# ScalarE takes the ranking's key copies, the index tiles' copies out of PSUM and the statistics of the last LayerNorm

## The chip, the cores and the metric

The kernel runs on one core of one Trainium2 chip, as one launch. The metric is the device time of that launch in microseconds, median of several runs. TensorE (PE) multiplies, VectorE (DVE) and ScalarE (ACT) work on tiles in SBUF and PSUM, GpSimd (POOL) issues the gathers of expert rows, SyncE (SP) issues the large loads and stores.

## What is computed

One layer of a streaming encoder for 1024 tokens of width 1024: an input projection with two mixers, a residual LayerNorm, and then a product-key expert layer (PEER) with another residual LayerNorm. The change touches only the expert layer and the last LayerNorm:

```python
def block(xb):                       # PEER
    q = (xb @ w_q).reshape(t, PEER_HEADS, 2, PEER_HALF)
    s = jnp.einsum('thpd,hpkd->thpk', q, sub_keys)
    s1, i1 = lax.top_k(s[:, :, 0], PEER_TOPK)
    s2, i2 = lax.top_k(s[:, :, 1], PEER_TOPK)
    cand_s = (s1[..., :, None] + s2[..., None, :]).reshape(t, PEER_HEADS, 256)
    cand_i = (i1[..., :, None] * PEER_N_KEYS + i2[..., None, :]).reshape(t, PEER_HEADS, 256)
    top_s, sel = lax.top_k(cand_s, PEER_TOPK)
    idx = jnp.take_along_axis(cand_i, sel, axis=-1)
    gate = jax.nn.softmax(top_s, axis=-1)
    act = jax.nn.gelu(jnp.einsum('thkd,td->thk', expert_u[idx], xb))
    return jnp.einsum('thk,thkd->td', gate * act, expert_v[idx])
...
x = LN(alpha * x + gate2(c) * PEER(h2)) * ln2_g + ln2_b
```

There are 8 heads, 128 keys a half, 16 chosen of each, and 16384 experts.

## The kernel before

**Two token sets.** The 1024 tokens are worked as set A (3 blocks of 128) and set B (5 blocks, 640 tokens). A's expert rows are gathered one by one from memory (GpSimd, `row_at` buffers) and multiplied in by VectorE (`u_row`, L1067, and `v_row`, L1076). B's experts are computed densely: TensorE multiplies B's tokens with all of `expert_u` (64 units "E") and, after a one-hot spread of the gates, with all of `expert_v` (64 units "W").

**Units.** All weights pass as units of 1 MB, in the order of the list UNITS: A's front (V, C, U, M, O), then B's with A's query units between (`B V`, `B C 0`, `A Q 0`, `B C 1`, ...), then `B U`, `B M`, `B O`, `B Q 0`, `B Q 1`, then five E units and one Q unit in turns up to `B Q 7`, then E 30 to E 63, then W. Every matrix product is three fp16 products (high by high, high by low, low by high). A unit is loaded into `stage` by SP, ScalarE writes its high part (`make_hi`, L726 to `w`), VectorE the low part (`make_lo`, L971), four units ahead of TensorE. For B a feature unit has 96 matmuls in 4 tiles of 24, 320 columns each; the tiles go round four PSUM banks, `psU`, so that TensorE may start a tile once ScalarE has copied out the tile four before it (`evacuate`, semaphore `tile_free`). The transposes, scores and spreads use four other banks, `psX`, released by `x_free`.

**Order.** There is no scheduler: each engine's program is written out in the loop over UNITS, and runs in that order. In each unit ScalarE copies the unit's tiles out, then the scores of the head before, then does `make_hi(n + 4)`, then the store of an E unit and the gelu of the row dots (`section_gelu`, which waits for VectorE's rows of two sections earlier). VectorE does `make_lo(n + 4)`, then some pieces of the ranking, then the rows of the unit (`rows_of`).

**Ranking.** `rank(x, h)` is a generator of six pieces for one head: piece 1 the first eight of 16 best scores, piece 2 the second eight and the indices as fp16 (`idx16`, L1318, which raises `sc_used`), piece 3 the first half of the best sums, piece 4 the second half and the places, and pieces 5 and 6 the lookup of the two indices: an `is_equal` of places with a counter (L1359), a multiplication with the indices (L1362), four additions. L1362 reads `idx16` with a broadcast last axis. In the E units head `1 + (u - 1) // 5` has pieces 1 and 2 at u % 5 == 1 and one piece in each unit after it; from u = 33 two. Head 0 of B has its first three pieces at `B Q 1` and the others at E 0.

**The way to the spread.** E_SPREAD is 40. After E 38 TensorE transposes six tiles (two index arrays and the gates, each in two parts) into `psX`, and VectorE copies them out (`idx_t`, L1413 and L1415) into `keys_t16` and `g_t`. From E 40 on VectorE makes one-hot tiles (`onehot_keys`, L1430, and `onehot_gate`, L1437; eight pairs a unit, q counts them), and TensorE multiplies them after the 9th and the 21st matmul of each tile (L1831). Gathers of the phase "spread" (from E 40) wait until the first L1430 is done.

**The end.** In `close(i, b)` VectorE finishes one block after the other, in the order 0, 1, 3, 4, 2, 5, 6, 7: it scales the sum (L1607 from SBUF for A's blocks, L1620 twice from PSUM for B's), adds the residual (L1622), takes the statistics (L1625, L996, L999), waits for ScalarE's square root (L756), and normalises (L1004, L1629, L1631). Three of B's ten output tiles share one PSUM bank and are copied out by `shared_out` (L1574), which releases the bank to TensorE.

## Time and profile before

| | us |
|---|---|
| median of three timed runs | 3033.12 (3030.32 to 3034.49) |
| the profiled execution | 3017.38 |
| its span, first to last instruction | 3015.6 |
| TensorE busy | 2903.5 |
| VectorE busy | 2554.3 |
| ScalarE busy | 836.3 |

The mean granted TensorE clock is 0.990 of full speed. A busy TensorE means here that matmuls follow one another; its idle stretches are few, and each has a row of its own in the timeline with the idle time and what ended it.

### The profile page before, as it was taken

The page shows a single profiled execution, that of the slowest core. Times are in us where ns is not written, and L with a number is a line of the kernel's source. Part 1 is how long each engine was busy: PE and PEld are TensorE (multiplying, and loading weights), DVE is VectorE, ACT ScalarE, POOL GpSimd, SP SyncE. Part 2 cuts the span into 40 slices and gives each one's busy share as a digit, 9 for nine tenths or more (in the row PEclk, how much of TensorE's full clock was granted, in tenths as well). Part 3 has the DMA queues.
Part 4 walks back from the last instruction along what each step waited for, and adds up shares of the span by engine and source line. Part 5 has one row for each costly group of instructions (what it writes and reads, how often), then busy time and mean ns, then how long its engine had stood idle before and what let it go on. Part 6 is the DMA issues. An engine that isn't in the chain of part 4 may idle for free.

```text
span 3015.6 us, 47305 instructions
## 1 busy us (share of the span) xinstructions
PE 2903.5 (96%) x19184; PEld 1916.8 (64%) x19184; DVE 2554.3 (85%) x4745; ACT 836.3 (28%) x1245; POOL 1007.8 (33%) x778
## 2 busy tenths in 40 slices
PE   4999999998999899999999899999999999999997
PEld 3666686676677776777777688888644444444443
DVE  5886557997887689999999888887699999999878
ACT  3333431211111422222223233333322222222220
POOL 0000000003775025555444422222366556555410
PEclk9999999999999999999999999999999999999999
DMA  8899644334999269888898888889899999999972
GB/s 329 336 350 369 213 171 164 128 105 182 393 393 358 91 238 340 315 329 333 316 351 305 299 287 294 285 285 294 334 415 415 410 399 406 398 409 401 348 276 104
DMA packets 266234, 917.53 MB, mean 304 GB/s; under 512 B 20464, under 2 KB 102432, under 8 KB 222752
## 3 DMA queue, kind: packets, MB, share of 16 engines
q1 hardware_dynamic: 63968, 427.91, 36.7%
q0 software_dynamic: 110592, 402.70, 35.5%
q10 hardware_dynamic: 91456, 83.89, 8.5%
q8 instruction: 152, 2.49, 0.3%
q14 instruction: 66, 0.54, 0.0%
HBM read 771.79 MB, written 142.63 MB: 303 GB/s over the span
## 4 chain that ended last, share of the span: by engine, by line
PE 54%; DVE 20%; issue 13%; DMA 10%; POOL 2%; ACT 1%; SPq 0%; DVEq 0%; ACTq 0%; POOLq 0%
PE psU L1651 11%; PE psU L1652 11%; PE psU L1653 11%; PE psX L1831 5%; PE psX L1651 5%; PE psX L1653 5%; PE psX L1652 5%; DVE acc_sp L1076 3%; DVE w L971 3%; DMA stage<-in_w_front 3%; DMA Z<-in_v_rows,idx_sp 2%; DMA rows<-in_v_rows,idx_sp 2%; DVE rows L1067 1%; POOL rows L719 1%; DMA rows<-in_u_rows,idx_sp 1%
## 5 line engine op out<-in xcount | busy, mean ns | idle before, releaser
L1651 PE MATMUL psU<-hB,w 128*128 128x320 f16 (+2 forms) x3104 | 931.7, 301 | 27.6 <-ACT Z L726 14.6
L1652 PE MATMUL psU<-hB,w 128*128 128x320 f16 (+2 forms) x3104 | 928.5, 300 | 0.0
L1653 PE MATMUL psU<-hB,w 128*128 128x320 f16 (+2 forms) x3104 | 928.2, 300 | 0.0
L971 DVE SCALAR_TENSOR_TENSOR w<-stage,w 128x2048 f16<-128x2048 f32 x176 | 402.8, 2289 | 115.6 <-ACT w L726 115.6
L726 ACT ACTIVATE w<-stage 128x2048 f16<-128x2048 f32 x176 | 335.9, 1909 | 544.1 <-PE psX L1653 349.5
L719 POOL DMA_INDIRECT rows<-in_u_rows,idx_sp x200 | 269.9, 1350 | 398.2 <-DVE rows L1067 253.1
L1651 PEld LDWEIGHTS psU<-hB,w 128*128 128x128 f16 x3104 | 308.5, 99 | 140.6 <-issue 20.6
L1653 PEld LDWEIGHTS psU<-hB,w 128*128 128x128 f16 x3104 | 305.4, 98 | 118.2
L1652 PEld LDWEIGHTS psU<-hB,w 128*128 128x128 f16 x3104 | 308.6, 99 | 111.2
L719 POOL DMA_INDIRECT rows<-in_v_rows,idx_sp x205 | 256.4, 1251 | 306.8 <-DVE rows L1067 209.3
L1651 PE MATMUL psX<-w,Z 128*128 128x512 f16 x768 | 291.1, 379 | 5.9 <-DVE Z L1574 4.3
L1652 PE MATMUL psX<-w,Z 128*128 128x512 f16 x768 | 291.1, 379 | 0.0
L1653 PE MATMUL psX<-w,Z 128*128 128x512 f16 x768 | 291.1, 379 | 0.0
L1651 PE MATMUL psU<-w,Z 128*128 128x512 f16 (+1 forms) x768 | 265.9, 346 | 9.6 <-DVE Z L1042 4.3
L1076 DVE SCALAR_TENSOR_TENSOR acc_sp<-rows,weight_sp,acc_sp 128x1024 f32<-128x1024 f32 x205 | 258.2, 1291 | 13.3 <-DMA rows<-in_v_rows,idx_sp 10.7
L1653 PE MATMUL psU<-w,Z 128*128 128x512 f16 (+1 forms) x768 | 265.8, 346 | 0.0
L1652 PE MATMUL psU<-w,Z 128*128 128x512 f16 (+1 forms) x768 | 265.7, 346 | 0.0
L1067 DVE SCALAR_TENSOR_TENSOR rows<-rows,h_sp 128x1024 f32<-128x1024 f32 x200 | 239.7, 1220 | 18.4 <-DMA rows<-in_u_rows,idx_sp 17.1
L726 ACT ACTIVATE R<-psU 128x320 f32<-128x320 f32 (+1 forms) x296 | 125.8, 429 | 424.7 <-PE psU L1653 424.4
L726 ACT ACTIVATE Z<-psU 128x320 f32<-128x320 f32 (+3 forms) x228 | 98.9, 447 | 471.7 <-PE psU L1653 423.8
L1651 PE MATMUL psU<-Z,w 128*128 128x384 f16 (+1 forms) x640 | 205.8, 322 | 0.0
L1652 PE MATMUL psU<-Z,w 128*128 128x384 f16 (+1 forms) x640 | 205.7, 321 | 0.0
(252 smaller groups left out, 4543.5 us busy)
## 6 DMA issues: line engine op xcount, KB each, us to landing
stage<-in_u_units SPq DMA_DIRECT2D x64, 1024.0 KB, 9.0
stage<-in_v_units SPq DMA_DIRECT2D x64, 1024.0 KB, 7.8
stage<-in_w_front SPq DMA_DIRECT2D x48, 1024.0 KB, 8.2
hl_dram<-w SPq DMA_DIRECT2D x48, 1024.0 KB, 6.3
w<-hl_dram SPq DMA_DIRECT2D x48, 1024.0 KB, 7.2
a_dram<-R ACTq DMA_DIRECT2D x64, 640.0 KB, 9.4
g_dram<-Z ACTq DMA_DIRECT2D x20, 2048.0 KB, 15.3
Z<-a_dram SPq DMA_DIRECT2D x32, 1280.0 KB, 11.6
```

What stands on the lines that cost most here:

```text
L719: pool.indirect_dma_start(row_at[r], None, u_rows if table == "u" else v_rows, bass.IndirectOffsetOnAxis(ap=idx_sp[:, slot:slot + 1], axis ...
L726: return nc.scalar.activation(dst, src, func, scale=scale)
L971: V.scalar_tensor_tensor(w[:, n % NW, 1, :], stage[:, v % 2, :], WS, w[:, n % NW, 0, :], ALU.mult, ALU.subtract).then_inc(lo_done, 1)
L1067: V.scalar_tensor_tensor(row_at[r], row_at[r], 1.0, h2_sp[:, slot % SB, :], ALU.mult, ALU.mult, accum_out=dots[:, c % 8, j:j + 1]).then_in ...
L1076: V.scalar_tensor_tensor(dst, row_at[r], weight_sp[:, slot:slot + 1], dst, ALU.mult, ALU.add).then_inc(row_used, 1)
L1651: mm(ps, lhs[0](k), rhs[0](k), start=start and s == 0, stop=False)
L1652: mm(ps, lhs[0](k), rhs[1](k), start=False, stop=False)
L1653: last = mm(ps, lhs[1](k), rhs[0](k), start=False, stop=stop and s == n - 1)
L1831: ins = mm(ps[:, t * P:(t + 1) * P], oh_keys[:, q % 4, 0, :, t], oh_gate[:, q % 4, c, :, t], start=(c == 0), stop=(c == 1))
```

## The change

Four edits, all in the programs of the engines:

1. **Keys.** A new `spread_keys` on ScalarE copies the 16 indices of each half into a full array `keys16` (16 by 16 a block), two ACTIVATEs a head: for A's heads 0 to 6 at the units of the table SPREAD_A, for B's head 0 at E 0, for B's head 1 + u // 5 at the E units with u % 5 == 2. It waits for `sc_used`, that is for the head's piece 2. VectorE multiplies with `keys16` instead of the broadcast `idx16`, after a wait on `keys_spread`; A's head 7 stays as it was.
2. **Index tiles.** ScalarE copies the six tiles out (`indices_out`): four after its `make_hi` at E 38, two in the middle of E 39. TensorE transposes four after E 38 and the two gate tiles inside E 39. VectorE's `idx_t` now stands after its rows of E 39 instead of before its rows of E 38.
3. **Rows.** In E 40 the first four pairs of one-hot tiles have no row between them; what is left of the rows follows at the unit's end.
4. **End.** `close` is cut in two: `close_sum` up to the residual, and `close` from the reciprocal on, done one block later. In between ScalarE makes the statistics: a Copy with its sum, the negative mean, a Square with its sum, and the square root.

```diff
+SPREAD_A = {("A", "Q", 1): 0, ("B", "C", 3): 1, ("A", "Q", 3): 2, ("B", "C", 6): 3, ("A", "Q", 5): 4,
+            ("B", "C", 9): 5, ("A", "Q", 7): 6}
...
+            def spread_keys(x, h):
+                k = rk[x]
+                act.wait_ge(sc_used, (HEADS if x == "B" else 0) + h + 1)
+                for half in range(2):
+                    dst = k["keys16"][:, half, :].rearrange("p (b j k) -> p b j k", b=NBLK[x], j=TOPK)
+                    activation(dst, k["idx16"][:, :, half, :].unsqueeze(3).to_broadcast([P, NBLK[x], TOPK, TOPK])
+                               ).then_inc(keys_spread, 1)
...
                 make_hi(n + NW)
+                if (x, kind, u) == ("B", "E", 0):
+                    spread_keys("B", 0)
+                if (x, kind, u) in SPREAD_A:
+                    spread_keys("A", SPREAD_A[x, kind, u])
+                if kind == "E" and u % 5 == 2 and u < E_SPREAD - 4:
+                    spread_keys("B", 1 + u // 5)
...
+                if (x, kind, u) == ("B", "E", E_SPREAD - 2):
+                    act.wait_ge(row_used, RANK_ROWS)
+                    indices_out(0, 4)
...
             for i, b in enumerate(CLOSE_ORDER):
-                root(R_END + i, slice(b, b + 1))
+                at, y = slice(b, b + 1), y_end[i % 2]
+                act.wait_ge(sum_ready, i + 1)
+                nc.scalar.activation(y, x_end[b], ACT.Copy, accum_out=total[:, at]).then_inc(act_step, 1)
+                act.wait_ge(act_step, 3 * i + 1)
+                activation(neg_mean[:, at], total[:, at], ACT.Copy, -1.0 / D).then_inc(act_step, 1)
+                act.wait_ge(act_step, 3 * i + 2)
+                nc.scalar.activation(y, x_end[b], ACT.Square, bias=neg_mean[:, at], accum_out=squares[:, at]
+                                     ).then_inc(act_step, 1)
+                act.wait_ge(act_step, 3 * i + 3)
+                nc.scalar.activation(std[:, at], squares[:, at], ACT.Sqrt, bias=end_eps[:, :], scale=1.0 / D
+                                     ).then_inc(std_ready, 1)
...
-                    step(V.tensor_tensor(cmp_t, cmp_t, k["idx16"][:, :, half, :].unsqueeze(3).to_broadcast([P, nb, TOPK, TOPK]),
-                                         ALU.mult))
+                    if (x, h) == ("A", HEADS - 1):
+                        keys = k["idx16"][:, :, half, :].unsqueeze(3).to_broadcast([P, nb, TOPK, TOPK])
+                    else:
+                        dve.wait_ge(keys_spread, 2 * (done - (x == "B")) - 1 + half)
+                        keys = k["keys16"][:, half, :].rearrange("p (b j k) -> p b j k", b=nb, j=TOPK)
+                    step(V.tensor_tensor(cmp_t, cmp_t, keys, ALU.mult))
...
-                        if q % 2:
+                        if q % 2 and q > 4:
                             next(rest, None)
...
-                if kind == "E" and u == E_SPREAD - 2:
-                    idx_t()
...
                     rows_of(unit)
+                    if kind == "E" and u == E_SPREAD - 1:
+                        idx_t()
...
-                step(V.scalar_tensor_tensor(x_end[b], x_end[b], ALPHA, y, ALU.mult, ALU.add))
-                settle()
-                for half in range(2):
-                    step(V.bn_stats(stats[:, b, half, :], x_end[b][:, half * HT:(half + 1) * HT]))
-                settle()
-                aggregate(range(b, b + 1), 2)
+                V.scalar_tensor_tensor(x_end[b], x_end[b], ALPHA, y, ALU.mult, ALU.add).then_inc(sum_ready, 1)
+
+            def close(i, b):
                 inverse(R_END + i, range(b, b + 1))
...
-                close(i, b)
+                close_sum(i, b)
+                if i:
+                    close(i - 1, CLOSE_ORDER[i - 1])
+            close(NB - 1, CLOSE_ORDER[-1])
```

ScalarE's program in E 1, E 2 and E 3, before (`R<-psU` are a unit's four tiles, `w<-stage` is `make_hi`, `dots` the gelu, the DMA the unit's store):

```order
L726 ACTIVATE R<-psU 128x320 x4
L929 DMA a_dram<-R 128x1280
L726 ACTIVATE dots<-dots 128x2
L726 ACTIVATE R<-psU 128x320 x4
L726 ACTIVATE w<-stage 128x2048
L929 DMA a_dram<-R 128x1280
L726 ACTIVATE dots<-dots 128x2
L726 ACTIVATE R<-psU 128x320 x4
```

and now:

```order
L974 DMA a_dram<-R 128x1280
L739 ACTIVATE dots<-dots 128x2
L739 ACTIVATE R<-psU 128x320 x4
L739 ACTIVATE w<-stage 128x2048
L739 ACTIVATE Z<-Z 128x1280 x2
L974 DMA a_dram<-R 128x1280
L739 ACTIVATE dots<-dots 128x2
L739 ACTIVATE R<-psU 128x320 x4
```

The two key copies of B's head 1 (`Z<-Z`) stand between `make_hi` of E 2 and the four tiles of E 3.

VectorE's program from its last rows of E 38 to the first one-hot tiles of E 40, before (L1067 and L1076 are rows, L1430 and L1437 the one-hot pair; the copies L1413 and L1415 and the casts L1419 to L1422 stand a few instructions further up, between `make_lo` and the rows of E 38):

```order
L1076 SCALAR_TENSOR_TENSOR acc_sp<-rows,weight_sp,acc_sp 128x1024 x2
L1089 SCALAR_TENSOR_TENSOR weight_sp<-dots,gate_sp 128x3
L1067 SCALAR_TENSOR_TENSOR rows,dots<-rows,h_sp 128x1024
L1067 SCALAR_TENSOR_TENSOR Z,dots<-Z,h_sp 128x1024
L1076 SCALAR_TENSOR_TENSOR acc_sp<-rows,weight_sp,acc_sp 128x1024 x2
L1089 SCALAR_TENSOR_TENSOR weight_sp<-dots,gate_sp 128x2
L1430 TENSOR_TENSOR Z<-Z 128x1024
L1437 TENSOR_TENSOR Z<-Z 128x1024
L1430 TENSOR_TENSOR Z<-Z 128x1024
L1067 SCALAR_TENSOR_TENSOR Z,dots<-Z,h_sp 128x1024
L1437 TENSOR_TENSOR Z<-Z 128x1024
```

and now:

```order
L1132 SCALAR_TENSOR_TENSOR acc_sp<-rows,weight_sp,acc_sp 128x1024 x2
L1145 SCALAR_TENSOR_TENSOR weight_sp<-dots,gate_sp 128x2
L1469 CAST Z<-Z 128x640
L1471 TENSOR_TENSOR Z<-Z 128x640
L1472 CAST Z<-iota_i 128x512
L1480 TENSOR_TENSOR Z<-Z 128x1024
L1487 TENSOR_TENSOR Z<-Z 128x1024
L1480 TENSOR_TENSOR Z<-Z 128x1024
L1487 TENSOR_TENSOR Z<-Z 128x1024
L1480 TENSOR_TENSOR Z<-Z 128x1024
```

The copies out of PSUM are gone from it, the rows come ahead of the casts, and no row stands between the first one-hot pairs.

ScalarE's last instructions are now, for the first and the second block:

```order
L1000 ACTIVATE Z,total<-Z 128x1024
L739 ACTIVATE neg_mean<-total 128x1
L1004 ACTIVATE Z,squares<-Z,neg_mean 128x1024
L1007 ACT_TABLE_LOAD
L1007 ACTIVATE std<-squares,end_eps 128x1
L1000 ACTIVATE Z,total<-Z 128x1024
L739 ACTIVATE neg_mean<-total 128x1
L1004 ACTIVATE Z,squares<-Z,neg_mean 128x1024
L1007 ACTIVATE std<-squares,end_eps 128x1
```

One table is loaded for all eight blocks.

## Rows read from the trace of the kernel before

**Rows 1.** The page's busy times: us, share of the span, instructions.

```profile
PE 2903.5 (96%) x19184; PEld 1916.8 (64%) x19184; DVE 2554.3 (85%) x4745; ACT 836.3 (28%) x1245; POOL 1007.8 (33%) x778
```

**Rows 2.** Timeline, TensorE: start, duration (us), instruction, idle time before it, releaser.

```profile
681.83 0.58 PE L1706 MATMUL psX<-Z,R 128*128 128x128 f32 x1 [4.05 <-DVE Z L1197]
...
1149.91 0.30 PE L1651 MATMUL psU<-hB,w 128*128 128x320 f16 x1 [2.91 <-ACT Z L726]
...
1679.42 0.77 PE L1847 MATMUL psX<-ident,Z 128*128 128x128 f32 x5 [4.64 <-DVE Z L1413]
...
1703.93 0.52 PE L1831 MATMUL psX<-Z 128*128 128x128 f16 x3 [4.34 <-DVE Z L1437]
...
2975.31 0.39 PE L1651 MATMUL psX<-w,Z 128*128 128x512 f16 x1 [3.10 <-DVE Z L1574]
...
3001.00 0.38 PE L1653 MATMUL psX<-w,Z 128*128 128x512 f16 x1
```

**Rows 3.** Busy time by stretches: length, PE, PEld, DVE, ACT, POOL, PEclk, DMA share, GB/s.

```profile
680.10:686.80 6.70, 4.97 (x20) 3.63 (x21) 4.09 (x9) 0.00 (x0) 0.00 (x0) 0.50 0.00 1
1151.20:1154.50 3.30, 3.30 (x14) 1.86 (x13) 3.06 (x18) 0.00 (x0) 0.53 (x1) 0.50 0.99 387
```

**Rows 4.** Groups by line and shape, VectorE: count, busy us, mean ns, idle before.

```profile
L1362 DVE TENSOR_TENSOR Z<-Z 128x1280 f16<-128x1280 f16 x16 | 23.9, 1492 | 0.6
L1362 DVE TENSOR_TENSOR acc_sp<-acc_sp 128x768 f16<-128x768 f16 x16 | 15.3, 958 | 0.6
L1359 DVE TENSOR_TENSOR Z<-Z,iota_jk 128x1280 f16<-128x1280 f16 x16 | 13.0, 814 | 0.1
L1359 DVE TENSOR_TENSOR acc_sp<-acc_sp,iota_jk 128x768 f16<-128x768 f16 x16 | 8.9, 558 | 0.6
```

**Rows 5.** The same of ScalarE.

```profile
L726 ACT ACTIVATE w<-stage 128x2048 f16<-128x2048 f32 x176 | 335.9, 1909 | 544.1 <-PE psX L1653 349.5 <-DMA stage<-in_w_front 121.0 <-DMA stage<-in_u_units 73.6
L798 ACT ACTIVATE hB<-Z 128x1024 f32<-128x1024 f32 x1 | 1.1, 1057 | 3.5 <-DMA Z<-in_c_row 3.5
```

**Rows 6.** Timeline, VectorE, in the rankings (columns as in rows 2).

```profile
643.53 0.17 DVE L1166 COPY Z<-carry 128x4 f32<-128x4 f32 x1 [2.63 <-ACT Z L726]
...
1128.57 0.24 DVE L1318 CAST Z<-Z 128x160 f16<-128x160 uint32 x1
...
1210.43 0.24 DVE L1318 CAST Z<-Z 128x160 f16<-128x160 uint32 x1
```

**Rows 7.** Timeline, ScalarE, in E 2, E 3 and at E 7.

```profile
1107.32 0.44 ACT L726 ACTIVATE R<-psU 128x320 f32<-128x320 f32 x1 [2.82 <-PE psU L1653]
1107.65 1.90 ACT L726 ACTIVATE w<-stage 128x2048 f16<-128x2048 f32 x1
...
1120.36 0.44 ACT L726 ACTIVATE R<-psU 128x320 f32<-128x320 f32 x1 [2.82 <-PE psU L1653]
...
1194.11 1.91 ACT L726 ACTIVATE w<-stage 128x2048 f16<-128x2048 f32 x1 [0.54 <-DMA stage<-in_u_units]
```

**Rows 8.** Timeline, VectorE, from `make_lo` at E 38 to the first one-hot tile.

```profile
1676.61 2.29 DVE L971 SCALAR_TENSOR_TENSOR w<-stage,w 128x2048 f16<-128x2048 f32 x1
...
1695.37 0.68 DVE L1430 TENSOR_TENSOR Z<-Z 128x1024 f16<-128x1024 f16 x1
```

**Rows 9.** The chain that ended last, two gathers: issued, us until landed.

```profile
1661.44 13.87 DMA rows<-in_v_rows,idx_sp
...
1687.78 6.30 DMA rows<-in_v_rows,idx_sp
```

**Rows 10.** Timeline, VectorE, the first block's end and the last instruction.

```profile
2954.50 1.23 DVE L1622 SCALAR_TENSOR_TENSOR Z<-Z 128x1024 f32<-128x1024 f32 x1
2955.76 1.29 DVE L1625 BATCH_NORM_STATS2 stats<-Z 128x6 f32<-128x512 f32 x2
...
2957.83 1.27 DVE L1629 SCALAR_TENSOR_TENSOR Z<-Z,mv,h_sp 128x1024 f32<-128x1024 f32 x1
...
3011.24 1.28 DVE L1631 SCALAR_TENSOR_TENSOR hB<-hB,rstd,h_sp 128x1024 f32<-128x1024 f32 x1
```

More of the change, by code:

```diff
@@ L320, in trunk_layer @@
         unread = sb("unread", [P, 1])
+        end_eps = sb("end_eps", [P, 1])
+        total = sb("total", [P, NB])
+        neg_mean = sb("neg_mean", [P, NB])
+        squares = sb("squares", [P, NB])
         dots = sb("dots", [P, 8, 12])
@@ L497, in trunk_layer @@
         sc_used = sem("sc_used")
+        keys_spread = sem("keys_spread")
         s_shift = sem("s_shift")
@@ L513, in trunk_layer @@
         v_free = sem("v_free")
+        sum_ready = sem("sum_ready")
+        act_step = sem("act_step")
         y_ready = sem("y_ready")
@@ L790, in scores, with indices_out @@
                     activation(flat[:, HT * i:HT * i + n], psX[a % 4][:, 0:n]).then_inc(x_free[a % 4], 1)
+            def spread_keys(x, h):
[5 more added lines that the diff above has]
+                               ).then_inc(keys_spread, 1)
+            def indices_out(lo, hi):
+                for i in range(lo, hi):
+                    kind, (first, last) = i // 2, SPLIT["B"][i % 2]
+                    a = X_IDX + i
+                    n, at = (last - first) * P, slice(first * P, last * P)
+                    wait_x(act, a)
+                    if kind < 2:
+                        activation(keys_t16[:, kind, at], psX[a % 4][:, 0:n]).then_inc(x_free[a % 4], 1)
+                    else:
+                        activation(g_t[:, at], psX[a % 4][:, 0:n], ACT.Copy, GS).then_inc(x_free[a % 4], 1)
             def section_gelu(n):
@@ L908, in _ @@
                             evacuate(t + 2 * j + half, slot[:, j, half * HB:(half + 1) * HB], ACT.Gelu_apprx_tanh)
+                            if u == E_SPREAD - 1 and 2 * j + half == 1:
+                                indices_out(4, 6)
                 if (x, kind, u) == ("A", "C", 5):
@@ L1118, in _ @@
             step(V.memset(modc[:, :], 0.0))
+            step(V.memset(end_eps[:, :], EPS))
             dve.wait_ge(tanh_c, 1)
@@ L1404, in idx_t @@
             def idx_t():
-                dve.wait_ge(row_used, RANK_ROWS)
-                for i in range(6):
-                    kind, (lo, hi) = i // 2, SPLIT["B"][i % 2]
-                    a = X_IDX + i
-                    n = (hi - lo) * P
-                    at = slice(lo * P, hi * P)
-                    wait_x(dve, a)
-                    if kind < 2:
-                        V.tensor_copy(keys_t16[:, kind, at], psX[a % 4][:, 0:n]).then_inc(x_free[a % 4], 1)
-                    else:
-                        V.tensor_scalar(g_t[:, at], psX[a % 4][:, 0:n], GS, None, ALU.mult).then_inc(x_free[a % 4], 1)
                 for i in range(4):
@@ L1764, in q_scores, with index_tiles @@
                     ins.then_inc(x_ready, 1)
+            def index_tiles(lo, hi):
+                for i in range(lo, hi):
+                    flat = (i1_all, i2_all, s_all)[i // 2]["B"].rearrange("p b h k -> p b (h k)")
+                    first, last = SPLIT["B"][i % 2]
+                    ps = x_tile(X_IDX + i)
+                    for b in range(first, last):
+                        ins = nc.tensor.transpose(ps[:, (b - first) * P:(b - first + 1) * P], flat[:, b, :], ident[:, :])
+                    ins.then_inc(x_ready, 1)
             pe.wait_ge(ident_ready, 2)
@@ L1834, in _, with gates_between @@
                     feature_unit(n, hl, spread)
+                elif (x, kind, u) == ("B", "E", E_SPREAD - 1):
+                    def gates_between(r, s):
+                        if (r, s) == (1, 2):
+                            pe.wait_ge(gate_ready, 2)
+                            index_tiles(4, 6)
+                    feature_unit(n, hl, gates_between)
                 else:
@@ L1839, in _ @@
                 if (x, kind, u) == ("B", "E", E_SPREAD - 2):
[L1840 to L1849 removed]
+                    pe.wait_ge(s_shift, 2)
+                    index_tiles(0, 4)
             first_w = N_OF["B", "W", 0]
```

16 lines of the change are left out of this document (4 added, 12 removed).

## The prediction

> **What bounds the kernel now.** I read the page's busy times first: TensorE is at 96% of the span, VectorE at 85%, ScalarE at 28% [rows 1]. So work that leaves VectorE shortens the kernel only where TensorE stands waiting for it, and work put on ScalarE costs only where TensorE comes to wait for ScalarE. The next view is TensorE's timeline with the idle time in front of each instruction. The waits that the edits can reach are few [rows 2]: 4.05 us at 681.83 (VectorE, the mixer's tiles), 2.91 at 1149.91 (ScalarE, which had not copied out a tile), 4.64 at 1679.42 (the index tiles in PSUM), 4.34 at 1703.93 (the second one-hot pair), 3.10 at 2975.31 (the shared PSUM bank). Behind such waits the granted clock is 0.50 for a while, 1.2 instead of 2.4 GHz [rows 3]: 3.3 us behind the wait that ends at 1149.91, which costs half of that, 1.65; behind the one that ends at 681.83 until 686.8, 5.0 us, which costs 2.5. Last, the end: TensorE's last matmul starts at 3001.00 [rows 2], VectorE's last instruction ends at 3012.52 [rows 10]. There VectorE sets the end.
>
> **Own time and median.** The sum is made on the profiled execution: span 3015.6, its time 3017.38. The median of the timed runs is 15.7 us higher, with no part of it in this view; I carry the difference over unchanged.
>
> **1. Keys on ScalarE, set A.** The multiplication with a broadcast operand takes 0.958 us at 768 columns and 1.492 at 1280; the comparison of the same size, with whole rows in its last axis, 0.558 and 0.814 [rows 4]. I take these for the new multiplication: 0.40 and 0.68 saved a half, 0.8 and 1.36 a head. Of A's seven heads nearly all of it is lost: at 643.53 VectorE has caught up and waits 2.63 us for tiles of TensorE's pace [rows 6]. Only head 6 comes after it, so VectorE comes 0.8 us earlier to the wait that ends at 681.83, and TensorE's next wait behind it is one for VectorE's chain as well. Term: **-0.8** (0 to -2, the latter if the slow clock gets shorter too).
>
> **2. Keys on ScalarE, set B.** ScalarE's 1024 columns take 1.057 us, its 2048 columns 1.909 [rows 5], so 0.832 ns a column; 1280 columns are 1.27, two copies about 2.5 us. In idle time they are free. But they stand behind a wait. At E 2 ScalarE is through with `make_hi` at 1107.65 + 1.90 = 1109.55 [rows 7] and now waits for `sc_used` of head 1. VectorE is two units behind here: that cast ends at 1128.57 + 0.24 = 1128.8 [rows 6], less 1.36 for head 0 is 1127.45. With the copies ScalarE is back at 1130.0. Queued behind it are the four tiles of E 3. TensorE finishes the fourth at 1120.2 (ScalarE's copy of it starts at 1120.36 [rows 7]) and can't start E 4 before the first is copied out, at 1130.5. **TensorE stands still for about 10.3 us**, and a slow clock of 1.65 to 2.5 follows; I take 2.1. What goes in return: VectorE catches up during the standstill, so the 2.91 us at 1149.91 and its 1.65 of clock are gone. Counted through: a unit of 96 matmuls takes 13.04 us (from the last tile's copy at 1107.32 to that at 1120.36 [rows 7]). E 4 and the query unit behind it take two times that, so E 5 starts at 1130.5 + 26.1 + 2.1 = 1158.7 instead of 1149.91 + 1.65 = 1151.55. Term: **+7.1** (+5.5 to +9). Head 0 at E 0 does not do this: ScalarE waits there about 5 us, with 3 us left before TensorE needs a bank. From E 5 to E 38 TensorE has no wait before and I expect none.
>
> **3. Index tiles and first one-hot pairs.** Before: 4.64 us of wait, 4.34 at the second pair [rows 2], and behind each the same 3.3 us of slow clock as behind the one at 1149.91, 1.65 of cost each: 12.3 in all with nothing between but E 39. Now TensorE passes E 38 without a stop: ScalarE frees the banks, and E 39 starts at 1674.7 and ends, with five transposes in it, at 1688.2, in the frame of the old trace. It wants the first pair at 1689.4. VectorE's `make_lo` of E 38 started at 1676.61 [rows 8] and can't be over 0.6 earlier, since ScalarE's half ends at 1676.0. Then come 2.2 us, the four rows of E 38, four rows of E 39, and the casts, 1.75. The rows of E 39 hang on gathers: the two of the nearest kind took 6.3 us in a quiet stretch and 13.9 under a 1 MB load [rows 9], and the gathers of E 39 are now issued while the load of that unit runs (1678 to 1687). I take 9 us for the first of the last three, issued at 1679.8, and 1.3 more for each next: rows done at 1692.2, casts at 1694.0, first pair at 1695.4 instead of 1696.8 (1695.37 and two instructions [rows 8]). So TensorE waits here again, some 6 us, with 2.2 of clock. The gain is the second pair: no row, which had waited for its gather, stands in front of it. It starts 2.6 us behind the first, and the point of full speed comes at 1695.5 + 2.6 + 2.2 = 1700.3 instead of 1703.93 + 1.65 = 1705.6. Term: **-5.3** (-2.5 with gathers of 13 us, -9 with gathers of 6 us and no slow clock).
>
> **4. The end.** Between L1625 and L1629 a block spends 2957.83 - 2955.76 = 2.07 us on VectorE [rows 10]; eight blocks are 16.6. Without it VectorE, which goes from 2954.50 to 3012.52, would be through at 2996, before the last matmul; so now TensorE sets the end. Its wait of 3.10 goes too (the shared tile was taken late by a busy VectorE): last matmul at 2997.9, done at 2998.1. Then the second half is scaled, 0.7, and L1622 takes 1.23: 3000.05. ScalarE: two passes of 1.06, two small ones of 0.2, hand-overs 0.3, 2.8 in all, beside which VectorE closes the block before (0.2 + 1.27 + 1.28). Then 2.75 for the last: 3005.6 instead of 3012.5. Term: **-6.8** (-5.5 to -7.5). The table load stands once, in the first block, where nobody is late.
>
> A rule speaks against this part. The Trainium skill, "ScalarE: Activation LUTs", section "Rules for kernel authors", gives multiplications and additions to VectorE, which by it is up to about three times faster per element in bf16. If ScalarE took three times the 2.07 us of the last block's statistics, the term would be -3.5 and the sum -2.5. The rows of ScalarE's passes [rows 5] speak for 2.8 us, and these tiles are fp32.
>
> **Sum:** -0.8 + 7.1 - 5.3 - 6.8 = **-5.8 us**, span 3009.8, and 3033.1 - 5.8 = **3027.3**. That is 0.19%; what a measurement of this kernel tells from no change is about 0.2%, 6.1 us.
>
> **Rivals.** (a) *The standstill at E 3 doesn't come.* For that `sc_used` of head 1 would have to come 10 us earlier against TensorE than 1127.45. Then the 4.6 us of old wait and clock shrink by up to VectorE's 2.7 us of savings: term about -3 instead of +7.1, sum -16, time 3017. Against it: VectorE's timeline has no idle time over 0.3 us from 1067 to 1192, so its cast hangs on its own work alone. Chance 0.10. (b) *The gathers eat the third term.* All of them land as late as the 13.9 us one; then the first pair comes near 1699, the second term stays, sum -2.5, time 3030.6. Nothing excludes it, since the load runs in that stretch; 0.22. (c) *Slower: ScalarE is caught at the next head as well.* At E 7 ScalarE is through at 1196.0 [rows 7], shifted by 7.1 at 1203.1; the cast ends at 1210.7 [rows 6] less 2.7, at 1208.0, copies until 1210.5. TensorE needs the bank at the end of E 8, about 1151.55 + 4 units + 2.5 for a head's scores + 7.1 = 1213.3, 2.5 us later. If VectorE loses more than that there, each us is a us of TensorE and from 2 us on with 1.65 to 2.5 of clock, and the heads of E 12 and E 17 can repeat it. To end 6 us above before it takes 12 us, three such stops. Against it: the first standstill itself gives the slack. 0.08. (d) *The multiplication doesn't get faster* with a whole operand: terms 1 and 2 get 0 and +8.4, sum -3.7, time 3029.4; 0.05. The case worked out has the other 0.55.
>
> **Numbers.** Likeliest: 3027.3. Its own bounds added at random are about 4 us to each side. The 80% range runs from 3020 ((a) left out) to 3033.5 ((b), (d), and the dear ends of the case itself; (c) left out). Faster by over 0.2% is below 3027.05: just under half of the main case and (a), 0.42. Slower by over 0.2%: 0.09. Within: 0.49.
>
> **What would show it.** In the profile after: L1362's successor at 0.56 and 0.81 us. ScalarE idle near 1110 to 1127 in front of the key copies, ended by VectorE, and a TensorE row of some 10 us idle near 1130, and no such row near 1150. No TensorE wait behind the transposes at E 38, one of 4 to 8 us at the first one-hot pair and none at the second. VectorE waiting for TensorE in the last three blocks, and its end some 7 us behind the last matmul. It would be wrong if the 10 us row is missing, if more rows with ScalarE as releaser stand at E 8 to E 20, or if a wait appears in A's stretch 480 to 660, where ScalarE now waits 5 to 8 us a head for VectorE and I leave TensorE 2 us or more of slack each time.

## The result

The change makes the kernel faster: 3010.95 us (3009.90 to 3013.82, four executions) against 3033.80 us (3030.32 to 3037.34), a ratio of 0.9924 with a 95% interval of 0.9904 to 0.9943. The prediction, 3027.3 us with a range from 3020 to 3033.5, missed it by 16 us. Two repeats of the same comparison, on two chips, gave 0.9921 (0.9897 to 0.9944) and 0.9889 (0.9852 to 0.9926).

The spans of the two profiled executions are 3015.6 and 3008.3 us: 7.3 us apart, not 22.9. The 16 us between these two differences are what this document is about.

### The profile after

The page's busy times [rows 1]: VectorE has 31.7 us less, ScalarE 51.1 us more.

```profile
PE 2899.3 (96%) x19184; PEld 1915.4 (64%) x19184; DVE 2522.6 (84%) x4708; ACT 887.4 (29%) x1321; POOL 1007.0 (33%) x778
```

TensorE's timeline at the places of [rows 2]: start, duration, instruction, idle time before it, releaser.

```profile
680.63 0.38 PE L1756 MATMUL psX<-Z,R 128*128 128x128 f32 x1 [3.26 <-DVE Z L1254]
...
1128.60 0.43 PE L1701 MATMUL psU<-hB,w 128*128 128x320 f16 x1 [9.81 <-ACT R L739]
...
1678.12 1.25 PE L1823 MATMUL psX<-ident,Z 128*128 128x128 f32 x10
...
1699.54 0.52 PE L1891 MATMUL psX<-Z 128*128 128x128 f16 x3 [5.36 <-DVE Z L1487]
...
2997.20 0.38 PE L1703 MATMUL psX<-w,Z 128*128 128x512 f16 x1
```

The wait near 681 is 0.8 us shorter. There is a stop of 9.81 us at 1128.60, with ScalarE as releaser, and none at 1149. The transposes of the index tiles at 1678.12 run through without a wait, the first one-hot pair waits 5.36 us, the second not at all, and the 3.10 us at 2975 are gone. Behind the long waits the clock is at its lower level, 1.2 GHz (columns as in [rows 3]):

```profile
1128.60:1131.00 2.40, 2.40 (x10) 1.32 (x11) 2.40 (x6) 2.40 (x4) 1.85 (x2) 0.50 0.47 29
1131.00:1133.00 2.00, 2.00 (x14) 1.33 (x13) 2.00 (x3) 0.33 (x2) 1.63 (x2) 0.83 0.80 273
...
1699.50:1702.00 2.50, 2.46 (x14) 1.82 (x15) 2.43 (x4) 0.60 (x1) 1.89 (x3) 0.50 0.38 70
1702.00:1704.50 2.50, 2.50 (x15) 1.77 (x14) 2.47 (x4) 0.00 (x0) 1.97 (x2) 0.50 0.92 308
```

ScalarE's timeline at E 2 (before: [rows 7]) shows where the stop comes from. ScalarE is through with `make_hi` at 1108.02, waits 17.59 us for the cast L1375, and copies out unit E 3's four tiles only at 1128.04.

```profile
1106.12 1.90 ACT L739 ACTIVATE w<-stage 128x2048 f16<-128x2048 f32 x1
1125.61 1.27 ACT L739 ACTIVATE Z<-Z 128x1280 f16<-128x1280 f16 x1 [17.59 <-DVE Z L1375]
...
1126.79 1.25 ACT L739 ACTIVATE Z<-Z 128x1280 f16<-128x1280 f16 x1
...
1128.04 1.40 ACT L739 ACTIVATE R<-psU 128x320 f32<-128x320 f32 x4
```

The groups by line and shape of the multiplication (L1424, before L1362 [rows 4]): 825 and 558 ns in place of 1492 and 958. The third row is head 7 of set A, which keeps the broadcast operand: 957 ns, as before.

```profile
L1424 DVE TENSOR_TENSOR Z<-Z 128x1280 f16<-128x1280 f16 x16 | 13.2, 825 | 0.6
...
L1424 DVE TENSOR_TENSOR acc_sp<-acc_sp,rows 128x768 f16<-128x768 f16 x14 | 7.8, 558 | 0.5
L1424 DVE TENSOR_TENSOR acc_sp<-acc_sp 128x768 f16<-128x768 f16 x2 | 1.9, 957 | 0.1
```

And the end, ScalarE's and VectorE's timeline in the last block (before: [rows 10]):

```profile
2999.61 1.06 ACT L1000 ACTIVATE Z<-hB 128x1024 f32<-128x1024 f32 x1 [7.38 <-DVE hB L1672]
...
3001.02 1.15 ACT L1004 ACTIVATE Z<-hB,neg_mean 128x1024 f32<-128x1024 f32 x1
...
3002.30 0.29 ACT L1007 ACTIVATE std<-squares,end_eps 128x1 f32<-128x1 f32 x1
```

```profile
2997.62 0.69 DVE L1670 SCALAR_TENSOR_TENSOR Z<-psX,h_sp 128x512 f32<-128x512 f32 x1 [3.69 <-PE psX L1703]
...
3004.00 1.28 DVE L1678 SCALAR_TENSOR_TENSOR hB<-hB,rstd,h_sp 128x1024 f32<-128x1024 f32 x1
```

VectorE now waits 3.69 us for TensorE, and its last instruction ends 8.1 us behind the start of TensorE's last matmul; before it was 11.5 us.

### The sum, term by term, on the two profiled executions

I cut both traces at the same three places: TensorE's first matmul of the scores with which the E units begin (`psX<-Z`, L1762 at 1063.43 before, L1812 at 1061.90 after; the expectations below call it the first query matmul), the first transpose of the index tiles (1673.52 and 1678.12), the last matmul.

| part | predicted | between the two traces |
|---|---|---|
| up to the E units (term 1) | -0.8 | -1.5 |
| E 0 to E 38 (term 2) | +7.1 | 616.2 - 610.1 = +6.1 |
| index tiles to the last matmul (term 3 and the wait of 3.10) | -5.3 - 3.1 = -8.4 | 1319.1 - 1327.5 = -8.4 |
| last matmul to the end (rest of term 4) | -6.8 + 3.1 = -3.7 | 11.1 - 14.6 = -3.5 |
| sum | -5.8 | -7.3 |

So the sum holds for these two executions. What does not hold is what the prediction says ahead of its terms: "The median of the timed runs is 15.7 us higher, with no part of it in this view; I carry the difference over unchanged". The changed kernel's profiled execution (3010.14 us) lies 0.8 us below its median, the one of before 16.4 us below.

### The profile page after: what moved, and what is told of

Its sections match the earlier page's. It is cut to its first block and busy times, and to the rows that moved or that the text cites. A ratio compares the mean times of both kernels' runs of the same rounds, so it can differ in the third digit from the quotient of the medians.

```text
span 3008.3 us, 47374 instructions
## 1 busy us (share of the span) xinstructions
PE 2899.3 (96%) x19184; PEld 1915.4 (64%) x19184; DVE 2522.6 (84%) x4708; ACT 887.4 (29%) x1321; POOL 1007.0 (33%) x778
## 5 line engine op out<-in xcount | busy, mean ns | idle before, releaser
L732 POOL DMA_INDIRECT rows<-in_u_rows,idx_sp x200 | 263.8, 1319 | 391.1 <-DVE rows L1123 250.3
## 6 DMA issues: line engine op xcount, KB each, us to landing
Z<-a_dram SPq DMA_DIRECT2D x32, 1280.0 KB, 11.5
```

The lines of the kernel that those rows point to most:

```text
L732: pool.indirect_dma_start(row_at[r], None, u_rows if table == "u" else v_rows, bass.IndirectOffsetOnAxis(ap=idx_sp[:, slot:slot + 1], axis ...
```

## The experiments

**Is the profile of before a typical one?** The kernel before was run again, unchanged, three times. All ratios here are estimates from all executions of both kernels, and can differ from the quotient of the two medians, by up to 0.0025.

> The kernel before, unchanged. The profiled span fell by 7.3 us with the change (3015.6 to 3008.3) but the medians by 22.9 us (3033.8 to 3011.0). Theory 1: the profiled execution of before was a lucky one and most executions have spans near 3031; then the spans here are 3028 to 3035 with one in some of 3016, and the extra 15 us stand as waits in some rows of TensorE. Theory 2: the kernel before is as long as its profile shows and the 16 us of the medians belong to other executions (another chip or another moment): then the spans here are 3014 to 3017 and the ratio of the change is 0.9976.

> One more trace of the kernel before. Between TensorE's first query matmul of the E units (near 1063) and its first one-hot pair the two traces so far take 633.4 and 651.8 us. If the second is the rule: 645 to 655 here, with four or more stops of 1 to 6 us between 1150 and 1690.

> The same once more: 645 to 655 us of E units if the long course is the rule, 633 to 637 if the short one is as common.

Theory 1 holds. The first run has a median of 3033.0 us beside 3033.5 (ratio 0.9993, 0.9974 to 1.0012). Its twelve executions have spans from 3012.3 to 3037.3 us, ten of them above 3025; the new traces have spans of 3035.4, 3038.5 and 3031.7. I call the time from TensorE's first score matmul (L1762) to its first one-hot pair (L1831) the **E stretch**. It took 633.4 us in the trace that the prediction used, and 651.8, 656.5 and 652.9 us in the three new ones. Up to the stretch and behind it they differ little from the old one (-2.5 to +0.4, and -0.9 to +2.1 us). The row of busy times over that stretch, before and before_again (TensorE, its weight loads, VectorE, ScalarE, GpSimd, clock, DMA share, GB/s):

```profile
1063.43:1696.84 633.41, 624.70 (x4601) 453.84 (x4601) 612.08 (x1698) 175.57 (x301) 305.40 (x237) 0.99 0.85 317
```

```profile
1063.78:1715.53 651.75, 627.09 (x4600) 454.33 (x4601) 612.06 (x1698) 170.01 (x301) 303.71 (x237) 0.99 0.83 307
```

VectorE's work is the same to 0.02 us. Its idle time is 21.3 us in one and 39.7 in the other. Whom it waits for, as sums by line between 1064 and 1680 (us in all, times, longest), first of before, then of before_again:

```profile
DVE acc_sp L1076 <- DMA Z<-in_v_rows,idx_sp: 4.0, 3, 2.5
DVE acc_sp L1076 <- DMA rows<-in_v_rows,idx_sp: 2.5, 2, 1.8
```

```profile
DVE acc_sp L1076 <- DMA rows<-in_v_rows,idx_sp: 11.7, 7, 2.9
DVE acc_sp L1076 <- issue: 7.8, 5, 2.6
...
DVE acc_sp L1076 <- DMA Z<-in_v_rows,idx_sp: 5.1, 4, 2.0
```

These are the row products, which wait for gathered rows ("issue" is a wait with no releaser in the trace; it is counted with them, as it stands on the same line). VectorE loses some 25 us to them where the other execution loses 7. How late it gets can be counted in the traces: when VectorE has the indices of head 7 (L1318), TensorE has done 40.4 to 40.7 units of 96 matmuls since the E units began (query units counted too) in the three long traces, and 39.3 in the short one. The way from there to TensorE goes through the loads of the units. SyncE issues a unit's load only when VectorE is through with the low part of two units before (`lo_done`, L564), ScalarE's `make_hi` waits for the load, and the copies out of PSUM stand behind it. ScalarE's waits for the loads, in before, in before_again, and in one of the runs with a stop further down, pause_again:

```profile
ACT w L726 <- DMA stage<-in_u_units: 63.1, 16, 12.8
```

```profile
ACT w L726 <- DMA stage<-in_u_units: 217.4, 31, 13.3
```

```profile
ACT w L726 <- DMA stage<-in_u_units: 3.9, 4, 1.4
```

TensorE's waits in before_again, the largest two of six between 1150 and 1680, and the one behind the transposes:

```profile
1640.76 0.42 PE L1651 MATMUL psU<-hB,w 128*128 128x320 f16 x1 [3.39 <-ACT R L726]
...
1673.90 0.43 PE L1651 MATMUL psU<-hB,w 128*128 128x320 f16 x1 [5.55 <-ACT R L726]
...
1698.05 0.47 PE L1847 MATMUL psX<-ident,Z 128*128 128x128 f32 x1 [8.02 <-DVE Z L1413]
```

Neither of the first two is in the trace of the prediction, and the third is 4.64 there [rows 2]. In front of the second, VectorE ends its low part at 1657.72, the load is issued at 1657.74 and lands at 1667.93, and ScalarE copies out only at 1673.34:

```profile
1655.44 2.28 DVE L971 SCALAR_TENSOR_TENSOR w<-stage,w 128x2048 f16<-128x2048 f32 x1
```

```profile
1667.96 1.91 ACT L726 ACTIVATE w<-stage 128x2048 f16<-128x2048 f32 x1 [12.17 <-DMA stage<-in_u_units]
...
1673.34 1.40 ACT L726 ACTIVATE R<-psU 128x320 f32<-128x320 f32 x4
```

**Which part of the change takes the 16 us away?** Each part alone on the kernel before.

```
end_only:   L1625, L996, L999 out of close(); ScalarE's two passes in
index_only: indices_out() on ScalarE, gate tiles in E 39, idx_t() behind rows_of(),
            no row between the first four one-hot pairs
keys_only:  spread_keys() and SPREAD_A, the multiplication from keys16
```

> The kernel before with the end's statistics on ScalarE and nothing else. By the sum's fourth term -6.8 us against the kernel before (ratio 0.9978), whatever the medians do elsewhere. If the 16 us that the medians lose beyond the profile sit in the end, it is -23 us (0.9925).

Measured: 3029.1 us beside 3033.5, ratio 0.9980 (0.9956 to 1.0004). As wide as before: 3006 to 3035.

> The kernel before with only the index tiles' part: ScalarE takes them out of PSUM, the tiles of scores come in E 39, the row products stand ahead of the casts, the second one-hot pair is made at once. By the profile after, the waits of 4.64 and 4.34 us give way to one of 5.4: -4 us with the slow clock (ratio 0.9987). If the 16 us that only the medians show sit here, -20 us.

Measured: 3029.9, ratio 0.9983 (0.9961 to 1.0006), 3007 to 3039. The medians are 4.3 and 3.6 us lower, of the order of the two terms, but both intervals include no change at all. Neither part touches the spread of the executions.

> The kernel before with only the keys spread by ScalarE. By the two terms on the keys +5 to +7 us (ratio 1.0020), since TensorE stands 9.8 us in unit E 4 and 2.9 us less at E 5. If the 16 us that only the medians show come from VectorE being late in the E units, and the change takes them away by giving VectorE 1.36 us a head, the time is 10 us below the kernel before (ratio 0.997).

Measured: 3022.2, ratio 0.9960 (0.9947 to 0.9973), and narrow in its five executions: 3020.2 to 3025.3. The keys, priced as a loss of 6 us, gain 11. TensorE does stand for 9.9 us at 1129.26, as the sum says, but from there to the transposes it has no wait over 0.5 us. By the medians the three parts alone add up to 19 us, of the 23 of the whole change.

**The changed kernel without the end.**

> The changed kernel with the end as it was before (statistics of the last LayerNorm on VectorE). By the fourth term +6.8 us against the changed kernel, 3017.8, if the end's gain does not depend on the rest. The difference to the run with only the keys (3022.2) is then what the index tiles' part is worth with VectorE on time: -4 us.

Measured: 3020.6 beside 3037.8, ratio 0.9957 (0.9938 to 0.9975). E stretch 637.8 us. From the first one-hot pair on it takes 6.0 us more than the changed kernel (1314.8 against 1308.8): the end's term again. The index tiles' part shows in that stretch too (1314.8 against 1320.0 in keys_only), but not in the ratios, 0.9957 and 0.9960.

**Stop or saving?** The keys do two things: VectorE saves 1.3 us a head, and TensorE stops once for 10 us, in which VectorE catches up. The next three kernels separate them. In two of them head 1's copies stand one unit later.

```diff
-                if kind == "E" and u % 5 == 2 and u < E_SPREAD - 4:
+                if kind == "E" and u in (3, 7, 12, 17, 22, 27, 32):
                     spread_keys("B", 1 + u // 5)
```

> The changed kernel, with the copies of set B's head 1 one unit later on ScalarE (behind unit E 3, not E 2); the other heads as they are. The 9.8 us stop of TensorE at 1128.60 should go and 2 to 3 us at E 5 come back. Theory S (what steadies the E units is the 1.36 us that VectorE saves with every head): 8 to 10 us below the changed kernel, 3001 to 3003, as narrow. Theory P (the stop itself lets VectorE catch up once, and that is what keeps it ahead of the gathers): most of the gain is given back in stops further on, 3008 to 3020 and a wide spread.

> The kernel before with only the keys on ScalarE, and head 1 of set B one unit later. Theory S: 8 to 10 us below the run with only the keys (3022.2), 3012 to 3014. Theory P: no better than that run, 3020 to 3030, and as wide as the kernel before.

Neither theory foresaw what the traces show: the stop did not go, it moved on to the copies of head 2 at E 7. TensorE's rows in head1_late and in keys_late:

```profile
1209.76 0.43 PE L1701 MATMUL psU<-hB,w 128*128 128x320 f16 x1 [9.36 <-ACT R L739]
```

```profile
1216.33 0.43 PE L1689 MATMUL psU<-hB,w 128*128 128x320 f16 x1 [9.95 <-ACT R L733]
```

The waits of 2.1 and 2.0 us at E 5 came back in front of it. E stretches of 640.7 and 642.1 us; the medians are 3019.8 (ratio 0.9957, 0.9935 to 0.9979) and 3033.6 (0.9992, 0.9975 to 1.0009). head1_late has the same ratio as no_end beside it, although it has the end's part too, and keys_late is 4 us below the kernel before where 20 were expected of theory S. For theory S that is a miss. Theory P is not tested by them, since the stop did not go.

The third has the stop and no saving: one line more in ScalarE's program than the kernel before.

```diff
                 make_hi(n + NW)
+                if (x, kind, u) == ("B", "E", 2):
+                    act.wait_ge(sc_used, HEADS + 2)
```

> The kernel before with one added wait and no other change: behind unit E 2 ScalarE waits for VectorE's cast of head 1, which stops TensorE for some 7 us (no copies follow) as in the changed kernel. Theory P: VectorE catches up once, the stops between 1230 and 1700 shrink, the time is below or near 3030 and narrow. Theory S: VectorE is still as dear as before with every head, falls behind again within two or three heads, and the time is 3033 + 7 + 2 of slow clock less the 2.9 us at E 5 = 3036 to 3042, as wide as before.

> The kernel before with the added wait of ScalarE behind E 2 and no other change. Its first trace took 638.3 us for the E units, as short as with the keys on ScalarE (636.8 to 639.0). If the stop alone keeps VectorE clear of the late gathers: 637 to 642 here. If the saving per head is needed too: 648 to 660.

> As the run before: 637 to 642 us if the stop alone is enough, 648 to 660 in this or the other one if not.

The E stretch takes 638.3, 639.4 and 639.4 us in the three traces: 12 to 18 us less than in the three long traces of the kernel before, by adding a wait of 9 to 10 us and taking nothing away. TensorE's row in pause_again, with nothing over 0.5 us from there to the transposes, and VectorE's waits there:

```profile
1125.75 0.42 PE L1653 MATMUL psU<-hB,w 128*128 128x320 f16 x1 [8.96 <-ACT R L726]
```

```profile
DVE w L973 <- ACT w L726: 12.8, 4, 5.8
DVE acc_sp L1078 <- DMA Z<-in_v_rows,idx_sp: 4.3, 2, 3.7
DVE acc_sp L1078 <- DMA rows<-in_v_rows,idx_sp: 2.0, 2, 1.1
```

VectorE has all the work of the kernel before (612.6 us busy in the stretch) and now even waits 12.8 us for ScalarE. On the chip of the last two the single times are 3018.5 and 3025.9 us, beside 3040.3, 3033.5 and 3032.6 for the kernel before. But the first run, with twelve executions, gave a median of 3033.2 beside 3037.8 (0.9987, 0.9971 to 1.0003), some 4.6 us, with an interval that includes no change. The same holds for keys_late. So the gain of the stop alone is shown in the E stretch of three traces, and not settled by the times. The traced execution of pause_only took 3036.0 us in spite of its short stretch: it comes to the E units only at 1077.04, 13 to 16 us later than the four traces of the kernel before. On that chip the kernel before was not traced, so how its executions divide between the two stretches is open.

**The saving without the stop, and a larger one.**

```diff
-                if kind == "E" and u % 5 == 2 and u < E_SPREAD - 4:
+                if kind == "E" and u < E_SPREAD - 4 and (u == 32 or u % 5 == 3 and u < 33):
```

> The changed kernel with the copies of heads 1 to 6 of set B one unit later on ScalarE (behind E 3, E 8, ... E 28; head 7 behind E 32), so that ScalarE isn't caught by a cast that is two units late. Moving head 1 alone moved the stop of TensorE to head 2 (9.5 us at 1209.76). Theory P (one stop is needed, because VectorE is too late to catch up by itself): no 10 us stop, but VectorE stays late, with stops of 1 to 4 us from 1230 on; 3010 to 3025 and wide. Theory S (1.36 us less a head is enough): no stop anywhere from 1150 to 1690, 3001 to 3003, narrow.

The small waits are back (1.6, 1.9 and 1.5 us from 1148 to 1475), VectorE waits some 33 us for gathered rows, and head 7's copies, which did not move, catch ScalarE: TensorE stands 9.28 us at 1619.38. E stretch 646.8 us, 8 to 10 us longer than in the three traces of the changed kernel. The times do not show that difference: the median is 3019.8 (eight executions; ratio 0.9909, 0.9875 to 0.9943) beside 3015.0 for the changed kernel there, but its ratio is 0.9921.

```diff
-                if kind == "E" and u % 5 == 2 and u < E_SPREAD - 4:
+                if kind == "E" and u % 5 == 3 and u < 33:
...
-                    if (x, h) == ("A", HEADS - 1):
+                    if h == HEADS - 1:
                         keys = k["idx16"][:, :, half, :].unsqueeze(3).to_broadcast([P, nb, TOPK, TOPK])
```

> The changed kernel with the copies of heads 1 to 6 of set B one unit later on ScalarE, and head 7's keys multiplied by VectorE itself, so that ScalarE waits for no late cast. With all heads one unit later the stop came at head 7 alone (9.4 us at 1619), and three small ones of 1.7 to 2.1 us stood before. Theory P (late VectorE stays late unless TensorE stops once for it): the stops are 5 to 8 us in all in pieces of 1 to 3, no piece of 9; the time is 2 to 5 us below the changed kernel, and the wait at the first one-hot pair 7 us or more. Theory S' (the saving alone is enough, the other stops were chance): none at all between 1150 and 1690, 8 us below the changed kernel. Rival: the gathers take what the stop gave back, same time as the changed kernel or up to 5 us above, wider.

> The changed kernel again, on the same chip as the next run and for comparison with it: 3010 to 3016. From the trace: the 10 us stop near 1130, no stop of TensorE over 1 us from there to 1690.

Measured: 3035.5 us for late_7self and 3020.6 for the changed kernel, with the kernel before at 3057.0 (ratios 0.9935, 0.9909 to 0.9961, and 0.9889, 0.9852 to 0.9926). The 10 us stop near 1140 is gone, and late_7self is 15 us slower than the changed kernel; between the two traces the E stretch alone is 13.5 us longer (650.3 against 636.8). TensorE's sums in late_7self, up to 1680, and VectorE's two largest for gathered rows:

```profile
PE psU L1701 <- ACT Z L739: 6.1, 4, 2.3
PE psU L1701 <- DVE w L1027: 1.6, 1, 1.6
```

```profile
DVE acc_sp L1132 <- issue: 12.6, 5, 2.6
...
DVE acc_sp L1132 <- DMA rows<-in_v_rows,idx_sp: 4.9, 7, 1.1
```

The E stretch is 650.3 us: VectorE's work is 10.6 us less than in before_again, and the stretch 1.5 shorter. Behind 1680 come waits of 5.4 and 12.6 us. Theory P is right that a late VectorE stays late, with small stops and a long wait at the first pair; that it would still be faster than the changed kernel was wrong, and the rival's "up to 5 us above" was too little.

> The kernel before without the multiplication by the keys in set B's eight heads (that part of the computation is left out; set A keeps it, and ScalarE gets no added wait). It takes 2 x 1.49 = 2.98 us a head from VectorE, against 1.36 by the change. If the kernel before is slow in most executions because VectorE is late in the E units and meets the gathers, there is no stop of TensorE left between 1150 and 1640, and the time is 3033 less some 20 = 3010 to 3014, narrow. If VectorE's load is not what does it, the time stays at 3033.

This kernel leaves out a part of the computation, so it tells only what VectorE's load costs. Measured: 3023.2 us beside 3046.9, ratio 0.9938 (0.9906 to 0.9971), though not narrow (3013 to 3046). Its E stretch is the shortest of all, 627.6 us, without a single stop of TensorE over 0.4 us from E 0 to the transposes. The busy row of the stretch:

```profile
1076.24:1703.85 627.61, 623.58 (x4600) 454.03 (x4601) 587.88 (x1682) 174.66 (x301) 297.25 (x237) 0.99 0.86 319
```

So, in one trace, the amount of VectorE's work does it too, if it is 24 us less. The 10.6 us of late_7self were not enough by themselves.

**The changed kernel again.**

> The changed kernel, unchanged, beside the kernel before on the same chip. If its executions are narrow because VectorE is kept on time in the E units: 3009 to 3014, with few above 3020, and the ratio 0.992. If the four executions known were lucky ones: a spread like that of the kernel before.

Measured: 3015.0 us beside 3046.9, ratio 0.9921 (0.9897 to 0.9944); seven of twelve executions from 3011.5 to 3015.7, the others up to 3030.0. "Few above 3020" was a miss, they are five, and the run beside late_7self, with 3020.6, lies above its 3010 to 3016 too. But the E stretches of the three traces of the changed kernel are 637.6, 638.9 and 636.8 us. What differs stands mainly ahead of them: the two later traces come to the E units at 1073.24 and 1072.34, the first at 1061.90.

| E stretch, us | kernels, in the order of their traces |
|---|---|
| no 10 us stop | before 633.4, 651.8, 656.5, 652.9; end_only 637.2; index_only 652.7; late_7self 650.3; no_mult 627.6 |
| stop at head 7 | all_late 646.8 |
| stop at head 1 or 2 | changed kernel 637.6, 638.9, 636.8; keys_only 639.0; no_end 637.8; pause_only 638.3, 639.4, 639.4; head1_late 640.7; keys_late 642.1 |

With an early stop the stretch lies within 5.3 us in ten traces, and VectorE is on time at head 7 in all of them (39.3 units, counted as above). ScalarE's waits for the loads go the same way: 1.4 to 6.1 us in all with the stop at head 1, 28 with it at head 2, 63 and 90 in the short traces of before and of end_only, 45 in no_mult, and 172 to 217 in the six others. Without it, at VectorE's full load, it is either near 635 or near 653, and the trace that the prediction used was one of the short ones. By the times these are rare: 5 of 41 executions of the kernel before, on the chip of the first four experiments, are under 3017 us.

The gathers themselves differ. Issues of gathers between 1230 and 1640, with their number and the median time to landing, in before_again and then in the profile after:

```profile
rows<-in_v_rows,idx_sp POOLq DMA_INDIRECT x47, 7.6
rows<-in_u_rows,idx_sp POOLq DMA_INDIRECT x42, 9.5
Z<-in_u_rows,idx_sp POOLq DMA_INDIRECT x36, 9.2
Z<-in_v_rows,idx_sp POOLq DMA_INDIRECT x31, 7.8
```

```profile
rows<-in_v_rows,idx_sp POOLq DMA_INDIRECT x49, 6.2
rows<-in_u_rows,idx_sp POOLq DMA_INDIRECT x42, 7.3
Z<-in_u_rows,idx_sp POOLq DMA_INDIRECT x36, 6.5
Z<-in_v_rows,idx_sp POOLq DMA_INDIRECT x31, 6.1
```

A gather is issued when VectorE gives a row buffer back. My reading is a loop: if VectorE is late, more of its gathers go out beside the 1 MB loads of the unit, land later, and VectorE is later still. Two links of it can be read in the traces. Landing is slower beside a load: of the gathers from 1230 to 1640 in before_again, the 53 that have a 1 MB load in flight for at least four fifths of their first 6 us take 11.9 us in the median, the other 103 6.7; in the profile after the 42 of that kind take 9.9, the other 116 6.2. Here too VectorE's lateness moves the loads themselves, as shown above. And the stop shortens the landings by itself: the same four medians as above are 6.2, 8.3, 7.1 and 6.4 us in pause_again, 6.1, 7.9, 6.6 and 6.6 in pause_third, with all of VectorE's work. No run moved the loads, so that the loop as a whole makes the long course is argued, not shown. Nor do the landings tell the two courses of the kernel before apart: in its short trace the four medians are 7.7, 9.5, 8.6 and 6.1 us, the last alone clearly shorter. Lateness at the start does not either: when VectorE has the indices of head 2, TensorE is at 10.3 units in that trace and at 10.7 in end_only, which are short, and at 10.5 to 10.8 in the three long ones (9.4 to 9.8 where the stop at head 1 came first). What sends one execution into the long course and another into the short one stays open.

## Why the prediction was wrong, point by point

**Own time and median: the step that failed.** "I carry the difference over unchanged." The difference was no constant beside the kernel. It was the E stretch, 18 to 23 us longer in the usual execution than in the traced one, and the change takes it away. Two things that I had should have stopped me. The traced execution lay 12.9 us below the lowest of three timed ones, which themselves lie within 4.2. And VectorE had only 21.3 us of idle time in 633.4, so there was little room for gathers that land later. The runs give another sum in its place, with the new traces as base: E stretch 637.6 against 653.7 (the mean of the three), -16.1; the rest behind it 1308.8 against 1319.5, -10.7; ahead of it -0.1. That is -27 between traces of different chips, where the medians say -22.9.

**Term 1** (-0.8): -1.5, of which 0.8 in the wait at 680.63, as worked out. In A's stretch, where a wait of TensorE would have been a sign of being wrong, ScalarE waits for VectorE seven times, 46.3 us in all and 8.6 at most, and TensorE has none.

**Term 2** (+7.1): the standstill came at the place, with the releaser and almost the length that the working gave: 9.81 us for 10.3, and no wait at 1149. Against the traced execution the term is +6.1. Against the usual execution it has the other sign: -16.1 for the whole stretch. The stop that I counted as pure cost lets VectorE catch up, and with the stop alone the stretch is short in three traces of three, though the times of that kernel leave its gain unsettled. The step that failed inside the term is "From E 5 to E 38 TensorE has no wait before and I expect none": in its usual course the kernel before has six or seven there, of 0.4 to 6.0 us, and ScalarE waits 197 to 217 us in all for loads that a late VectorE holds back, in place of 63.

**Term 3** (-5.3): -5.1, if TensorE's 3.3 us at the shared bank are counted with the end. The wait at the first pair is 5.36 us for "some 6", none at the second. In index_only, where VectorE is late, it is 10.2 us, and 12.6 in late_7self: the term too is only right for a VectorE on time.

**Term 4** (-6.8): -3.45 behind the last matmul (14.57 to 11.12 us) and -3.3 at the shared bank, -6.7. ScalarE needs 2.98 us for a block's statistics, from 2999.61 to 3002.59, where I had 2.8 and VectorE took 2.07. The Trainium skill ("ScalarE: Activation LUTs", section "Rules for kernel authors") gives multiplications and additions to VectorE, in bf16 up to about three times faster per element. On these fp32 tiles the trace gives a factor of 1.4, 2.98 against 2.07 us, and ScalarE's work lies beside other work in seven of eight blocks, so the rule did not decide here. The alternative sum in that passage is 0.1 off: three times 2.07 us makes the term -3.4 and the sum -2.4.

**Rivals.** (a), the standstill doesn't come: it did. (b), the gathers eat term 3: not in the three traces of the changed kernel, with 4.65 to 6.42 us at the first pair and none at the second (its sum of -2.5 takes -2.0 for the term, where the term itself says -2.5 for gathers of 13 us). (c), ScalarE caught at E 7 as well: not in the changed kernel; head1_late has that stop in place of the one at E 2, and none follows it. (d): the multiplication is as fast as predicted, 825 and 558 ns for 814 and 558. None of them had the time right, since all four stood on the same carried difference. The chance of "faster by over 0.2%" doesn't add up either: (a) and just under half of the main case make 0.37, not 0.42.

## What to carry to other kernels

Before a sum is made on one traced execution, see whether that execution is a usual one, and take a second trace where the timed runs lie further from it than from each other: part of the kernel may run in two ways. Here it was the stretch in which VectorE has 3 to 6% of idle time and waits for gathers whose issue hangs on VectorE itself. And its lateness comes back on TensorE through loads that wait for it. In such a stretch a wait can pay: with one stop of 9 to 10 us, and nothing else changed, it was some 15 us shorter than the mean of the long traces, though the times of that kernel showed a gain of only 4.6 us, within the noise. A saving on VectorE without the early stop was tried in two sizes, with one trace each. 24 us less work made the stretch 24 to 29 us shorter than in the three long traces, 10.6 us less made it 1.5 to 6.2 shorter.

## What the runs showed of the hardware beside this

TensorE has short waits with no releaser, 0.3 to 1.7 us each, between matmuls of one group from 690 to 980 us. They are absent in the traces before and after, in those of the chip of the first four experiments and in those of the last chip (before_third, before_fourth, pause_again, pause_third), and add up to 3.8 to 13.5 us in each trace of three other chips, whatever the kernel. One of them in after_third, and the stretch around it with the DMA engines' share at 1.03:

```profile
734.56 0.30 PE L1701 MATMUL psU<-hB,w 128*128 128x320 f16 x1 [0.71 <-issue]
```

```profile
733.50:741.00 7.50, 5.26 (x34) 2.79 (x32) 5.81 (x8) 0.87 (x2) 6.20 (x5) 1.00 1.03 416
```

The granted clock is 1.00 there, so it is not the clock. In before and after the DMA share over 733 to 960 is 0.98 and 0.99 too, without such waits; so full queues are not enough to explain them, and their cause stays open. In the changed kernel they go with a later start of the E units (1073.24 and 1072.34 against 1061.90), and the medians differ between the chips as well: 3033, 3038, 3047 and 3057 us for the kernel before on four of them, 3015 and 3021 for the changed kernel on the last two of these. The change gains 32 and 36 us there, where the first comparison gave 23. Why it gains more is not shown, since the kernel before was traced on none of the three chips with such waits.
